# The last stores of a decoder step: one residual product, four vector adds, the sample rows and one store change their place

## The chip, the cores and the metric

The kernel runs on one core of a Trainium2 chip. The metric is the device time of one execution in microseconds (us). A core has TensorE (PE: matmuls, with its own weight loads, PEld), VectorE (DVE), ScalarE (ACT), GpSimd (POOL) and SyncE (SP), which here issues most DMAs. Every engine works through its own list of instructions in order and waits on semaphores; the program is over when all of them have reached the closing barrier.

## The reference, cut to what matters

One layer of a decoder is computed for 512 prompt tokens and 8 sample tokens (`D_MODEL` = 1024, all fp32): token mixing with sparse attention and gating, then a mixture of 32 experts with two experts for each token. Only the last sum touches the change:

```python
xp = xp + gate1 * merge_branches(...)                       # x2 in the kernel
xp = xp + gate2 * hierarchical_moe(modulate(xp, ...), ...)  # output y_prompt, (1, 512, 1024)
xs = xs + gate2 * hierarchical_moe(modulate(xs, ...), ...)  # output y_sample, (8, 1, 1024)
# hierarchical_moe: each token's output is the gated sum of its two experts' outputs
```

## The kernel before, in words

After token mixing the kernel sorts (token, choice) pairs into blocks of 64 rows, one expert each (`N_MAIN` = 35 blocks, and overflow blocks that run only where an expert got too many tokens). For each block POOL gathers the rows, PE computes gate, up and down products, DVE scales the result (`y_scaled`, L2697) and POOL scatters it to DRAM (`expert_rows`), into one place for each token and choice. 34 blocks are scattered so; the last one (label `LAST_LABEL`) isn't fetched back from DRAM for the prompt rows, but added by matmuls.

The end of the kernel, which the change touches, goes like this (t counts the four prompt tiles of 128 tokens, h the two halves of 512 columns):

- SP, once the scatters have landed (L1465), issues eight loads of 512 KB, `picked[c][t]` for choice c and tile t (L1468), in the order t = 0 to 3, and for each t choice 1, then choice 0. Behind them it waits for the last scatter (`s_scattered`) and issues two small loads of the sample rows (L1471, `s_picked`).
- PE adds the residual `x2` and the last block's rows in PSUM: `last_residual(t, h)` (L1337) is a product of the identity with `x2`, 128 rows by 512 columns; `last_tile(t)` calls `last_rows` (L1341) for both halves, products of a one-hot 64-row matrix with the last block's output, in the upper and the lower half of the array. Each fp32 product shows as two MATMUL records. `last_rows` of t = 0 waits for `y_out` of the last block (L1367), that is for DVE's L2697. Tile 3 is filled and drained by halves.
- ACT copies each finished tile from PSUM back into `x2` (L1687: tiles 0 to 2 whole, tile 3 by halves).
- DVE adds the two picks of a tile (`picks_summed(t)`, L2751), then the tile that ACT copied (`last_added(t)`, L2756; for tile 3 by halves, L2769). `last_added` first waits for all marked DVE operations before it (`lane.wait()`). Behind these come three small operations that make the sample rows (L2774 to L2776, 128 x 64): sum of the two choices, times gate, plus residual.
- SP stores tiles 0 to 2 (L1474), the halves of tile 3 (L1478) and the sample rows (L1480), each when its sum is ready, and waits for all to land before it goes to the closing barrier.
- PE, ACT, POOL and SP also run `over_pairs` (L587): a loop of two turns (L590) whose body, the overflow blocks, is skipped by a branch (L591) where there are none. PE runs it at its very end, after it has waited for ACT to drain every bank of the last tiles (L1379); ACT runs it at its end too; POOL after the last scatter (L1640); SP before the loads of L1468.
- L278 is the helper line of the closing barrier: a DRAIN on every engine, then the semaphores on which they meet.

The order in every engine's list is written out by hand.

Of the kernel before, what the change touches and what calls it, by code (L numbers as in the profile page):

```python
# [20 lines left out]
ALU = mybir.AluOpType  # L21
# [7 lines left out]
NT = SEQ // P  # L29
# [246 lines left out]
def decoder_step(nc, io):  # L276
    ctx = ExitStack()
    with ctx:  # L278
# [3 lines left out]
        def sem(name):  # L282
            return ctx.enter_context(nc.semaphore(name))
# [13 lines left out]
        def at(offset, size):  # L297
            return arena[:, offset:offset + size]
# [123 lines left out]
        s_cols = at(5120, 4 * Q_S).rearrange("p (m n) -> p m n", m=4)  # L422
# [69 lines left out]
        s_picked = (const2_in, 32 + 32)  # L492
# [6 lines left out]
        s_back = (x_in[NT], 16 + 32)  # L499
# [18 lines left out]
        outs, y_outs = sem("outs"), sem("y_outs")  # L518
# [44 lines left out]
        y_s_ready = (new_spread_ready, 2)  # L563
# [14 lines left out]
        def sample_columns(rows):  # L578

            return rows.rearrange("b (q n) -> (b q) n", q=16)  # L580
# [6 lines left out]
        def over_pairs(engine, pair):  # L587

            n_steps = engine.value_load(step_count[0:1, 0:1], min_val=0, max_val=N_OVER_STEPS)
            with engine.Fori(0, N_OVER_STEPS) as i:  # L590
                with engine.If(i < n_steps):  # L591
                    for q in range(OVER_AT_ONCE // 2):
                        pair(lambda per_pair, more: i * (per_pair * OVER_AT_ONCE // 2) + (per_pair * q + more))
# [13 lines left out]
        def pair(b0):  # L607

            return psum[:, b0:b0 + 2, 0:HALF]
# [7 lines left out]
        def _(pe):  # L617
# [415 lines left out]
            for g in range(2):  # L1033
                for h in range(2):
                    a = 2 * g + h
# [229 lines left out]
            def down(p, w, full):  # L1265
                for f in range(2):
                    for half in range(2):
                        mm = pe.matmul(psum[SB * half:SB * half + SB, 6 + p, :], hidden_T[:, p, f, :],  # L1268
                                       w[:, f, 512 * half:512 * half + 512], start=(f == 0), stop=(f == 1),
                                       tile_position=(0, SB * half))  # L1270
                mm.then_inc(full, 1)
# [8 lines left out]
            for b in range(N_SCATTERED + 1):  # L1280
                p = b % 2
                if b < N_SCATTERED:
                    pos, _, first, _ = BLOCKS[b]
                    if first:
                        pe.wait_ge(gu_got[pos % BUFFERS], 16 * (pos // BUFFERS + 1))
                    pe.wait_ge(xT_out, b + 1)
                    if b >= 2:
                        pe.wait_ge(hidden_done, b - 1)
                    if b == 3:
                        over_items()  # L1290
                    gate_up(p, w_gu[pos % BUFFERS], gu_full)
                    if b == 0:
                        gate_items()
                        over_code()
                    elif b == 2:
                        over_sums()
# [11 lines left out]
                if b >= 1:  # L1308
                    pos, _, first, _ = BLOCKS[b - 1]
                    if first:  # L1310
                        pe.wait_ge(dn_got[pos % BUFFERS], 16 * (pos // BUFFERS + 1))
                    pe.wait_ge(hT_out, b)
                    if b == 2:
                        banks.wait_drained(pe, "gate_items")
                    if b >= 3:
                        pe.wait_ge(y_out, b - 2)
                    down(1 - p, w_dn[pos % BUFFERS], y_full)
# [14 lines left out]
            def last_residual(t, h):  # L1332

                if h == 0 or t == NT - 1:
                    name = ("last", t, h) if t == NT - 1 else ("last", t)
                    banks.begin(pe, name, *((LAST_BANK[t] + h,) if t == NT - 1 else (LAST_BANK[t], LAST_BANK[t] + 1)))
                pe.matmul(psum[:, LAST_BANK[t] + h, :], ident, x2[:, t, 512 * h:512 * h + 512], start=True, stop=False)  # L1337
# [6 lines left out]
            def last_tile(t):  # L1344
                last_rows(t, 0)
                banks.filled(last_rows(t, 1), ("last", t))
# [14 lines left out]
            pe.wait_ge(y_out, b - 1)  # L1361
            down(LAST_P, w_dn[k], y_full)
            last_residual(1, 0)


            pe.wait_ge(last_hot_ready, 3)
            pe.wait_ge(y_out, N_MAIN)  # L1367
            last_tile(0)
            last_residual(1, 1)
            last_tile(1)  # L1370
            for h in range(2):
                last_residual(2, h)
# [11 lines left out]
        def _(sp):  # L1384
# [87 lines left out]
            for t in range(NT - 1):  # L1472
                sp.wait_ge(y_ready, t + 1)
                sp.dma_start(io["y_p"][t * P:(t + 1) * P, :], picked[0][t]).then_inc(y_outs, 16)  # L1474
            for h in range(2):
                cols = slice(512 * h, 512 * h + 512)
                sp.wait_ge(y_ready, NT + h)
                sp.dma_start(io["y_p"][(NT - 1) * P:NT * P, cols], picked[0][NT - 1][:, cols]).then_inc(y_outs, 16)  # L1478
            sp.wait_ge(*y_s_ready)
            sp.dma_start(sample_columns(io["y_s"]), s_cols[:, 2, :]).then_inc(y_outs, 16)  # L1480
            sp.wait_ge(y_outs, 16 * (T5 + 1))

        @block.gpsimd
        def _(pool):
            lane = Lane(pool, pool_lane)
# [186 lines left out]

            pool.wait_ge(over_ready, 1)
            over_pairs(pool, pool_pair)
            pool.wait_ge(outs, 16 * n_outs[0])

        @block.scalar
        def _(act):
# [59 lines left out]
            def products_out(name):  # L1738
                width = max(o + w for _, o, w, _ in slices[name])
                evac((name, "s"), [(G[:, 1, 0:width], psum[:, 2, 0:width])])  # L1740
# [168 lines left out]
            for i, (_, n, t) in enumerate(ORDER):  # L1909
                if i == 0:  # L1910
                    banks.wait_full(act, ("adaS", 8))
                square_half(i, n, t, 0, x2_half)
                if i == 3:
                    banks.wait_full(act, ("O0", "S"))
                    evac(("O1", "s"), [(G[:, 1, :], psum[:, 2, :])])
# [116 lines left out]
        def _(dve):  # L2032
            lane = Lane(dve, vector_lane)
# [662 lines left out]
            def y_scaled(p, done):  # L2696
                dve.tensor_tensor(y_rows[:, p, :], psum[:, 6 + p, :], y_rows[:, p, :], ALU.mult).then_inc(done, 1)  # L2697
# [50 lines left out]
            def picks_summed(t):  # L2748
                for c in (1, 0):
                    dve.wait_ge(*picked_in[c][t])  # L2750
                lane.mark(dve.tensor_tensor(picked[0][t], picked[0][t], picked[1][t], ALU.add))  # L2751

            def last_added(t):
                banks.wait_drained(dve, ("last", t))
                lane.wait()
                dve.tensor_tensor(picked[0][t], picked[0][t], x2[:, t, :], ALU.add).then_inc(y_ready, 1)  # L2756

            dve.wait_ge(y_full, b + 1)
            y_scaled(LAST_P, y_out)
            for t in range(NT):  # L2760
                picks_summed(t)
                if t < NT - 1:
                    last_added(t)
            for h in range(2):
                cols = slice(512 * h, 512 * h + 512)
                banks.wait_drained(dve, ("last", t, h))
                if h == 0:
                    lane.wait()
                dve.tensor_tensor(picked[0][t][:, cols], picked[0][t][:, cols], x2[:, t, cols], ALU.add).then_inc(y_ready, 1)  # L2769

            a, gate2, x = s_cols[:, 2, :], s_cols[:, 0, :], s_cols[:, 1, :]
            dve.wait_ge(*s_back)
            dve.wait_ge(*s_picked)
            lane.then(dve.tensor_tensor(a, a, s_cols[:, 3, :], ALU.add))  # L2774
            lane.then(dve.tensor_tensor(a, a, gate2, ALU.mult))
            dve.tensor_tensor(a, a, x, ALU.add).then_inc(y_s_ready[0], 1)  # L2776


# [90 lines left out]
```

## Time and profile before

| | us |
|---|---|
| device time, median of 3 runs | 794.43 (794.12 to 795.21) |
| device time of the profiled execution | 794.43 |
| its span, first to last instruction | 792.7 |
| PE busy | 744.3 (94%) |
| DVE, ACT, POOL busy | 407.6, 210.9, 169.6 |
| granted TensorE clock, mean | 0.985 |

The span is what the trace covers; about 1.8 us of the device time lie around it. Times in the rows are us from the span's start, where not marked ns. A row such as `773.47 1.13 PE L1337 ... x2` says: from 773.47, busy for 1.13 us, two instructions of line 1337. Names with a q behind the engine (SPq, PEldq) are what the engine's sequencer does itself: waits, branches, register loads, DMA issues.

### The profile page before, as it was taken

The numbers are of one execution on the slowest core, as the hardware profiler recorded it, in microseconds if no ns is written. First come the engines' busy times: TensorE is split into PE (matmuls) and PEld (weight loads), VectorE is DVE, ScalarE is ACT, GpSimd is POOL, SyncE is SP. The second block draws the span as 40 slices with busy tenths as digits, with TensorE's granted clock in tenths as the row PEclk, the third lists the DMA queues.
The fourth block names the chain that finished last, engine by engine and source line by source line (L and its number), as shares of the span: only waits on it lengthen the run. The fifth ranks groups of instructions, "written<-read, shape, count | busy, mean of one in ns | idle before, by whom it ended". The sixth has DMA issues, their size and how long they took to land.

```text
span 792.7 us, 11139 instructions
## 1 busy us (share of the span) xinstructions
PE 744.3 (94%) x4235; PEld 457.9 (58%) x4235; DVE 407.6 (51%) x940; ACT 210.9 (27%) x426; POOL 169.6 (21%) x193
## 2 busy tenths in 40 slices
PE   4999999999999989999999999987999999999886
PEld 3444465588766656887888344555555555555431
DVE  4124299998999989600214523883433232232225
ACT  4013243415366866103000211221111111111102
POOL 2030012051000000064400002454233333333210
PEclk9999999999999999999999999997999999999999
DMA  8962032533056444243132822148999999999987
GB/s 343 420 192 93 1 106 74 212 120 111 27 211 239 162 172 159 98 154 137 61 107 80 342 110 107 55 171 358 421 431 422 422 429 424 424 427 419 425 335 274
DMA packets 26832, 183.80 MB, mean 232 GB/s; under 512 B 6960, under 2 KB 7384, under 8 KB 15384
## 3 DMA queue, kind: packets, MB, share of 16 engines
q1 hardware_dynamic: 16328, 161.06, 50.2%
q0 software_dynamic: 9536, 19.72, 7.5%
q10 hardware_dynamic: 912, 2.26, 0.8%
q8 instruction: 36, 0.59, 0.3%
q14 instruction: 20, 0.16, 0.1%
HBM read 178.66 MB, written 14.44 MB: 244 GB/s over the span
## 4 chain that ended last, share of the span: by engine, by line
PE 79%; DMA 9%; ACT 4%; DVE 4%; issue 2%; POOL 1%; SPq 0%; DVEq 0%; POOLq 0%; ACTq 0%
PE psum L764 22%; PE psum L1254 13%; PE psum L731 11%; PE psum L1268 7%; DMA arena<-in_experts 5%; PE psum L695 3%; PE psum L641 3%; PE psum L1247 2%; DMA ring<-in_stream 2%; ACT arena L1687 2%; DMA arena<-in_cache_ki,stat 1%; PE psum L1155 1%; PE psum L949 1%; PE psum L624 1%; PE psum L960 1%
## 5 line engine op out<-in xcount | busy, mean ns | idle before, releaser
L764 PE MATMUL psum<-hT,ring 128*128 128x260 f32 x640 | 143.8, 384 | 0.9 <-issue 0.5
L1687 ACT ACTIVATE arena<-psum 128x512 f32<-128x512 f32 (+10 forms) x135 | 73.1, 576 | 236.0 <-PE psum L764 56.4
L764 PEld LDWEIGHTS psum<-hT,ring 128*128 128x128 f32 x640 | 120.5, 190 | 23.6 <-issue 4.4
L731 PE MATMUL psum<-ring,hT 128*128 128x512 f32 (+1 forms) x256 | 94.6, 523 | 0.0
L731 PEld LDWEIGHTS psum<-ring,hT 128*128 128x128 f32 x256 | 47.8, 192 | 43.7 <-issue 34.9
L1254 PE MATMUL psum<-ring,arena 128*64 128x256 f32 x608 | 70.7, 386 | 1.9 <-DMA ring<-in_experts 1.2
L1268 PE MATMUL psum<-arena 128*64 128x512 f32 x280 | 67.8, 605 | 1.4 <-issue 1.4
L1619 POOL DMA_INDIRECT expert_rows<-arena,router x34 | 34.5, 1014 | 142.0 <-DVE arena L2697 129.7
L1254 PEld LDWEIGHTS psum<-ring,arena 128*64 128x64 f32 x608 | 44.5, 140 | 32.2 <-issue 11.3
L2690 DVE COPY arena<-psum 128x128 f32<-128x128 f32 x35 | 10.2, 291 | 98.2 <-PE psum L1261 80.1
L1980 ACT ACTIVATE arena<-psum 64x256 f32<-64x256 f32 x35 | 13.4, 382 | 172.2 <-PE psum L1254 92.5
L764 PE MATMUL psum<-arena,ring 128*128 128x260 f32 x256 | 58.6, 391 | 0.0
L764 PEld LDWEIGHTS psum<-arena,ring 128*128 128x128 f32 x256 | 49.6, 194 | 7.9
L2697 DVE TENSOR_TENSOR arena<-psum,arena 128x512 f32<-128x512 f32 x35 | 24.2, 691 | 47.3 <-PE psum L1268 47.3
L1548 POOL DMA_INDIRECT arena<-in_cache_k,arena x16 | 15.4, 960 | 148.6 <-DVE arena L2331 141.2
L1254 PE MATMUL psum<-arena 128*64 128x256 f32 x352 | 40.0, 380 | 2.5 <-DMA arena<-in_experts 1.7
L1613 POOL DMA_INDIRECT arena<-t_rows,router x35 | 35.9, 1026 | 17.9 <-issue 10.1
L2194 DVE MAX8 arena<-arena 40x8 f32<-40x1025 f32 x32 | 38.7, 1211 | 0.7 <-issue 0.2
L2195 DVE FIND_INDEX8 arena<-arena 40x8 uint32<-40x1025 f32 x32 | 38.8, 1211 | 0.0
L2196 DVE MATCH_REPLACE8 arena<-arena 40x1025 f32<-40x1025 f32 x32 | 38.5, 1204 | 0.0
L1254 PEld LDWEIGHTS psum<-arena 128*64 128x64 f32 x352 | 25.5, 137 | 19.8 <-issue 5.6
L1268 PEld LDWEIGHTS psum<-arena 128*64 128x64 f32 x280 | 17.1, 136 | 27.7 <-issue 27.4
(395 smaller groups left out, 953.7 us busy)
## 6 DMA issues: line engine op xcount, KB each, us to landing
ring<-in_stream SPq DMA_DIRECT2D x21, 2048.0 KB, 8.3
ring<-in_experts SPq DMA_DIRECT2D x16, 2048.0 KB
arena<-in_experts SPq DMA_DIRECT2D x32, 1024.0 KB
arena<-in_experts SPq DMA_DIRECT2D x11, 2048.0 KB
hT<-in_experts SPq DMA_DIRECT2D x5, 2048.0 KB
ring<-expert_rows SPq DMA_DIRECT2D x8, 512.0 KB, 7.7
ring<-in_stream SPq DMA_DIRECT2D x2, 1280.0 KB, 6.0
arena<-in_x_prompt SPq DMA_DIRECT2D x4, 512.0 KB, 6.0
```

The lines of the kernel that those rows point to most:

```text
L641: mm = pe.matmul(psum[32 * j:32 * j + 32, b, :], c_T[:, 4 * h + j, :], w[:, 4 * h + j, :], start=(h == 0), stop=(h == 1), tile_position=(0 ...
L731: mm = pe.matmul(psum[:, b, 0:width], hT[:, k, t * P:(t + 1) * P], w[:, k, :], start=(k == 0), stop=(k == KD - 1))
L764: mm = pe.matmul(psum[:, b0 + s, 0:HALF], w[:, k, f * P:(f + 1) * P], rhs[:, k, s * HALF:(s + 1) * HALF], start=(first and k == 0), stop=( ...
L1254: mm = pe.matmul(psum[SB * half:SB * half + SB, 2 + p, 0:DE], x_T[:, p, k, :], w[:, 4 * (k % 2) + k // 2, col:col + DE], start=(k == 0), s ...
L1268: mm = pe.matmul(psum[SB * half:SB * half + SB, 6 + p, :], hidden_T[:, p, f, :], w[:, f, 512 * half:512 * half + 512], start=(f == 0), sto ...
L1613: pool.indirect_dma_start(x_rows[:, b % X_BUFFERS, :], None, half_rows, bass.IndirectOffsetOnAxis(token_tab[:, label:label + 1], 0), bound ...
L1619: pool.indirect_dma_start(picks, bass.IndirectOffsetOnAxis(dest_tab[:, label:label + 1], 0), y_rows[:, b % 2, :], None, bounds_check=4 * T ...
L1687: ins = act.activation(out, in_, func, scale=scale)
L2194: lane.then(dve.max(best, s))
L2195: lane.mark(dve.max_index(idx_u[0:32 + NS, 8 * r:8 * r + 8], best, s))
L2196: lane.then(dve.match_replace(s, best, s, TAKEN))
L2697: dve.tensor_tensor(y_rows[:, p, :], psum[:, 6 + p, :], y_rows[:, p, :], ALU.mult).then_inc(done, 1)
```

## The change

Five edits, all in the last 20 us:

- PE: `last_residual(1, 1)` moves from behind `last_tile(0)` to ahead of the wait for `y_out`, so that it follows `last_residual(1, 0)`.
- DVE: the order of picks sums (P) and last adds (A) by tile, before P0 A0 P1 A1 P2 A2 P3, becomes P0 P1 P2 A0 A1 P3 A2; the two halves of tile 3 follow as before.
- The three operations of the sample rows leave DVE's list and stand in POOL's, behind its `over_pairs`, with their waits.
- SP: the store of the sample rows moves ahead of the stores of tile 3's halves, with its wait for `y_s_ready`.
- Semaphores and buffers stay as they were.

```diff
             down(LAST_P, w_dn[k], y_full)
             last_residual(1, 0)
+            last_residual(1, 1)
 
             pe.wait_ge(last_hot_ready, 3)
             pe.wait_ge(y_out, N_MAIN)
             last_tile(0)
-            last_residual(1, 1)
             last_tile(1)
...
                 sp.dma_start(io["y_p"][t * P:(t + 1) * P, :], picked[0][t]).then_inc(y_outs, 16)
+            sp.wait_ge(*y_s_ready)
+            sp.dma_start(sample_columns(io["y_s"]), s_cols[:, 2, :]).then_inc(y_outs, 16)
             for h in range(2):
...
-            sp.wait_ge(*y_s_ready)
-            sp.dma_start(sample_columns(io["y_s"]), s_cols[:, 2, :]).then_inc(y_outs, 16)
...
             over_pairs(pool, pool_pair)
+
+            a, gate2, x = s_cols[:, 2, :], s_cols[:, 0, :], s_cols[:, 1, :]
+            pool.wait_ge(*s_back)
+            pool.wait_ge(*s_picked)
+            lane.then(pool.tensor_tensor(a, a, s_cols[:, 3, :], ALU.add))
+            lane.then(pool.tensor_tensor(a, a, gate2, ALU.mult))
+            pool.tensor_tensor(a, a, x, ALU.add).then_inc(y_s_ready[0], 1)
...
-            for t in range(NT):
-                picks_summed(t)
-                if t < NT - 1:
-                    last_added(t)
+            picks_summed(0)
+            picks_summed(1)
+            picks_summed(2)
+            last_added(0)
+            last_added(1)
+            picks_summed(3)
+            last_added(2)
+            t = NT - 1
             for h in range(2):
...
-
-            a, gate2, x = s_cols[:, 2, :], s_cols[:, 0, :], s_cols[:, 1, :]
-            dve.wait_ge(*s_back)
-            dve.wait_ge(*s_picked)
-            lane.then(dve.tensor_tensor(a, a, s_cols[:, 3, :], ALU.add))
-            lane.then(dve.tensor_tensor(a, a, gate2, ALU.mult))
-            dve.tensor_tensor(a, a, x, ALU.add).then_inc(y_s_ready[0], 1)
```

## Rows read from the trace of the kernel before

**Rows 1.** Chain that ended last, from 784 us: start, duration, what.

```profile
783.90 1.07 PE psum L1341 x2
...
786.74 0.23 DVE arena L2776
```

**Rows 2.** Waits of SP, from 765 us: total us, times, longest.

```profile
SPq L278 <- PEq L278: 2.6, 1, 2.6
SPq L278 <- DMA out_y_s<-arena: 2.5, 1, 2.5
```

**Rows 3.** Line 278, the closing barrier: duration ns min/median/max, first and last start.

```profile
L278 POOLq DRAIN  x1: 9303/9303/9303, 777.4 to 777.4; - x1
...
L278 SPq COMPARE_BRANCH  x1: 37/37/37, 789.9 to 789.9; - x1
...
L278 PEldq DRAIN  x1: 8/8/8, 792.4 to 792.4; - x1
```

**Rows 4.** Lines 589 and 591, loop count and skipping branch, same columns.

```profile
L589 PEldq TENSOR_LOAD <-router x1: 1080/1080/1080, 785.7 to 785.7; - x1
...
L591 ACTq COMPARE_BRANCH  x2: 50/52/55, 786.2 to 787.1; - x2
L591 PEldq COMPARE_BRANCH  x2: 232/2076/3920, 787.4 to 791.9; - x2
```

**Rows 5.** Timeline of PE from 773 us: start, busy, engine, line, what.

```profile
773.47 1.13 PE L1337 MATMUL psum<-arena,const 128*128 128x512 f32 x2
774.52 1.13 PE L1341 MATMUL psum<-arena 64*128 64x512 f32 x4
775.58 1.13 PE L1337 MATMUL psum<-arena,const 128*128 128x512 f32 x2
...
777.70 1.98 PE L1337 MATMUL psum<-arena,const 128*128 128x512 f32 x4
779.61 1.13 PE L1341 MATMUL psum<-arena 64*128 64x512 f32 x4
```

**Rows 6.** Timeline of DVE and ACT, 774 to 787 us; in brackets idle and releaser.

```profile
774.19 1.22 DVE L2751 TENSOR_TENSOR ring<-ring 128x1024 f32<-128x1024 f32 x1
...
776.75 1.23 DVE L2756 TENSOR_TENSOR ring<-ring,arena 128x1024 f32<-128x1024 f32 x1 [1.35 <-ACT arena L1687]
...
784.99 0.60 ACT L1687 ACTIVATE arena<-psum 128x512 f32<-128x512 f32 x1 [1.51 <-PE psum L1341]
...
785.62 0.69 DVE L2769 TENSOR_TENSOR ring<-ring,arena 128x512 f32<-128x512 f32 x1 [0.62 <-ACT arena L1687]
786.23 0.22 DVE L2774 TENSOR_TENSOR arena<-arena 128x64 f32<-128x64 f32 x1
```

**Rows 7.** Timeline of SP's DMA issues, same columns.

```profile
782.37 1.74 SPq L1474 DMA_DIRECT2D out_y_p<-ring  x3
...
787.00 0.36 SPq L1480 DMA_DIRECT2D out_y_s<-arena  x1
```

**Rows 8.** Lines 1468 and 1471: issue ns, first and last start, and time to landing.

```profile
L1468 SPq DMA_DIRECT2D ring<-expert_rows x8: 341/440/943, 769.0 to 772.4; - x8
...
DMA to landing us min/median/max: 3.8/7.7/9.9
...
L1471 SPq DMA_DIRECT2D arena<-expert_rows x2: 319/376/432, 781.5 to 781.9; - x2
...
DMA to landing us min/median/max: 1.6/1.8/1.9
```

**Rows 9.** Windows of and behind the stores: us, busy of PE, PEld, DVE, ACT, POOL, clock, DMA share, GB/s.

```profile
783.30:788.90 5.60, 1.66 (x4) 0.29 (x2) 2.87 (x6) 0.78 (x2) 0.00 (x0) 1.00 1.00 383
...
788.90:792.70 3.80, 0.00 (x0) 0.00 (x0) 0.00 (x0) 0.00 (x0) 0.00 (x0) 0.57 0.03 6
```

**Rows 10.** POOL's groups of instructions: count, busy us, mean ns, idle before.

```profile
L1572 POOL TENSOR_TENSOR arena<-arena 128x1024 f32<-128x1024 f32 x4 | 9.4, 2346 | 4.2 <-DVE arena L2460 4.2
...
L1581 POOL TENSOR_TENSOR router<-router 128x1 f32<-128x1 f32 x4 | 0.8, 191 | 0.3
```

## The prediction

> **What bounds the kernel now.** I read the chain of waits first, because all five edits lie in the last 20 us. It follows TensorE up to the last product of line 1341 (783.90 to 784.97), then ScalarE's copy and VectorE, and stops at the third sample operation at 786.74 [rows 1]. Taken at its word, the sample rows and the store behind them are the end. But the span is 792.7, so nearly 6 us lie behind the chain's last piece, and the chain doesn't say whose they are. So the second view is what SP waits for. It waits 2.5 us for the last store, and then 2.6 us more for TensorE's sequencer at the closing barrier [rows 2]. The third view, the barrier's own line, puts times to it: SP leaves its wait for the stores at 789.9, TensorE reaches its DRAIN only at 792.4, and 0.2 us later all is over [rows 3]. TensorE is the last engine, by about 2.3 us.
>
> What does TensorE do after its last product? Its wait for ScalarE's last copy (784.99 plus 0.60) [rows 6] ends at 785.6; then comes the register load for the loop count (1.08 us from 785.7), and at 787.4 the branch that skips the overflow blocks, which takes 3.92 us; its second branch takes 0.23. ScalarE's same two branches take 0.05 each [rows 4]. So the end is made of this chain: last product, ScalarE's copy, and a tail of 792.4 - 785.6 = 6.8 us in TensorE's sequencer. Stores, VectorE and the sample rows run beside that tail.
>
> **The change part by part.** The sums are made against the profiled execution: span 792.7, device time 794.43, which happens to be the median too, so 1.8 us outside the span are carried over unchanged.
>
> *PE, one residual product earlier.* From 773.47 TensorE never stops: each group starts as the one before lets it, 1.05 to 1.06 us apart where full-array products (1337) and half-array products (1341) alternate [rows 5]. The wait for `y_out` costs nothing today: VectorE's L2697 is through at 774.3, while the residual of 773.47 runs to 774.52. With two residual products ahead it is further off the path. No product is added or taken away. What changes is who stands beside whom. Two residual groups side by side exist in the rows: the pair of 777.70 gives way to the next group at 779.61, 1.91 us, where two separate ones take 2 x 1.055 = 2.11. One such pair more saves 0.20 us. The edit also puts `last_tile(0)` beside `last_tile(1)`, half-array groups back to back, which these rows don't show. Bounds: nothing gained or lost, if their alternating weights keep the 1.06 us; 0.20 gained, if it is like the residual pair. I take 0.20, since the nearest row is that pair and the number of changes between the two kinds falls from four to two there. Sum on TensorE: 0.20 + 0.20 = 0.40 us, range 0.20 to 0.40. The last product ends at 784.57. Tile 0 is filled 0.85 us later than before, tile 1 0.2 to 0.4 earlier.
>
> The Trainium skill, TensorEngine Tiling (Array Packing), section Key Properties, says that a change of tiling mode drains the array. By this rule the tile pair saves the same 0.20 us as the residual pair, and the sum is 0.40; without it 0.20. The rows' 2.11 against 1.91 agree with it.
>
> *ScalarE.* Its copies follow TensorE; the last moves from 784.99 to 784.6 and ends at 785.2 [rows 6]. Nothing else enters its list.
>
> *TensorE's tail.* Same instructions, same count in front of the branch, 6.8 us, so its DRAIN comes at 792.0. The one thing that can stretch it is the 3.92 us branch. The stores are in flight beside it: from 783.3 to 788.9 the DMA engines are fully busy at 383 GB/s [rows 9]. The Trainium skill, Runtime: NRT & Kernel Launch, section Instruction fetch mechanics, says that a taken branch to code outside the window held forces a DMA fetch before execution goes on; the branch's 3.92 us against 0.05 on an engine with a short body [rows 4] agrees. By this rule the stall depends on DMA traffic, and I price that as a rival below.
>
> *VectorE, new order.* A picks sum needs two loads of 512 KB. The eight land between 769.0 + 3.8 = 772.8 and 772.4 + 9.9 = 782.3 [rows 8], one every 9.5/7 = 1.36 us; so the pairs are complete at about 774.2, 776.9, 779.6 and 782.3. In the old order A0 (776.75) fills the gap between them [rows 6]. In the new one P1 runs from about 777 and P2 from 779.7 to 780.9, with VectorE idle in between, and only then A0 (to 782.3), A1 (to 783.4), P3 (to 784.6), A2 (784.7 to 785.9), the halves at 785.8 and 786.4, the last done at 787.1. Before, it was 785.62 + 0.69 = 786.3. So the last prompt sum comes 0.8 us later, although three operations of 0.22 us leave VectorE's list. Who waits for that is SP alone.
>
> *POOL.* Its three operations wait for the sample loads: 781.9 + 1.9 = 783.8 [rows 8]. POOL is free since 777.4 [rows 3]. No row has a 128 x 64 one. Lower bound 0.19 us each (128 x 1), upper 2.35 us each (128 x 1024) [rows 10]. I go between them by size, 0.19 + 2.16 x 64/1024 = 0.33, with a small gap 1.1 us in all: ready at 784.9. Upper end: 783.8 + 7.1 = 790.9.
>
> *SP.* Two waits change place. The sample store now stands ahead of tile 3's halves, and its wait holds both of them. New times: A0 at 782.4, A1 at 783.4, A2 at 785.9 (the three stood behind one another from 782.37 to 784.1), sample rows 786.4 (was 787.0) [rows 7], halves 786.8 and 787.2. The stream then has 1.05 MB left from A2 on; at 383 GB/s that is 2.7 us, from some 1 us after its issue: 787.0 to 789.7, landed by 790.2, perhaps 790.8. Before, 789.9. So SP reaches the barrier 0.3 to 0.9 us later, but still 1.2 us or more before TensorE's 792.0. Cost zero, and the cover is TensorE's tail; without it this part would be a loss of 0.3 to 0.9 us.
>
> Sum: 792.7 - 0.4 = 792.3 span, and 794.43 - 0.40 = **794.0 us** of device time. That is 0.05%. A measurement of this kernel can tell about 0.2% (1.6 us) from no change, so the forecast is "no measurable change".
>
> **The rivals.**
>
> 1. *The stores set the end* (the chain's picture). Then the time follows the last landing, 0.3 to 0.9 us later by the sum above: 795.0. For it: the chain stops in the sample rows [rows 1]. Against it: SP's 2.6 us wait for TensorE [rows 2]. Chance 0.05.
>
> 2. *The branch meets the store stream.* It now starts at 787.0 instead of 787.4, and the stream ends at 789.7 instead of 788.9. If what the branch fetches waits behind the stores, it ends 0.8 us later than before instead of 0.4 earlier: 794.43 + 0.8 = 795.2. For it: the branch spans the end of the stream. Against it: the 2.4 us of the branch that lie behind 788.9 are spent on an idle DMA system [rows 4, 9], so most of the stall is no queueing. Chance 0.12.
>
> 3. *The slower side: POOL is late.* The three operations at their upper end are ready at 790.9; SP, blocked in front of tile 3's halves, then issues three stores, the last landing about 3.0 us later, 793.9, and SP is in the barrier at 794.1 instead of TensorE at 792.0. Against the old 792.4 that is +1.7: 796.1. It decides over TensorE from a ready time of about 788.8, which is 1.7 us for each operation, and loses against the kernel before from 789.2. For it: POOL's DRAIN of 9.3 us in the old tail, ending only at 786.7 [rows 3], which no row explains; if it blocked the three operations too, they would be ready at 787.8, and SP would be in the barrier at about 791.1: still no loss. Against it: 0.19 us for a small operation [rows 10]. Chance 0.06.
>
> The Trainium skill, GPSIMD Engine Reference, section Key points, says that POOL's SBUF interfaces are shared with VectorE where VectorE has two SBUF inputs, as all its sums here have. By this rule the operations stretch towards rival 3, and no row here prices a 128 x 64 one beside such sums.
>
> 4. *The tail shrinks*: the fetch finds the code or the branch is short, up to 3.7 us off TensorE, when the stores become last at 790.8: 794.43 - 1.6 = 792.8. Nothing in the list of TensorE speaks for it. Chance 0.03.
>
> **How the numbers follow.** Forecast 0.74: 794.0, its own range 793.6 to 794.5. Rivals 1 and 2 (0.17) lie at 795.0 and 795.2 and are within 0.2% too, as the forecast is. Rival 3 reaches 796.1 only at its far end. The range takes the forecast with rivals 1 and 2 and the scatter of the runs shown: 793.4 to 795.4. Faster by over 0.2%: rival 4 and scatter, 0.06. Slower by over 0.2%: the far end of rival 3 and scatter, 0.07. Between them 0.87.
>
> **What would show it.** TensorE: two residual groups at 773.5 to 775.4, two tile groups behind them in 1.9 us, the last product at 784.6, its DRAIN last at about 792.0, SP again waiting for it, now 1.2 to 1.8 us. VectorE: idle before the second and the third picks sum, its last sum done near 787.1. POOL: three operations of some 0.3 us from 783.8. SP: tile 2's store at 785.9. Wrong would be: SP's or POOL's DRAIN last; a branch that isn't within 0.5 us of 3.9; tile groups 1.06 us apart; or device time outside 793.4 to 795.4.

## The result, and the profile after

The changed kernel is slower: 798.09 us median (796.3 to 803.18, 17 runs) against 794.43 (791.22 to 797.62, 17 runs) of the kernel before; ratio 1.0053, 95% interval 1.0038 to 1.0067. The forecast was 794.0 and "no measurable change"; both the size and the range were missed.

One thing is needed to read the traces. The time ahead of the change differs from run to run: VectorE's last `y_scaled` ends anywhere from 767.9 us (e6) to 776.6 us (e8) in traces whose lists are alike up to the last blocks, so a span by itself says little. I therefore count from the end of this `y_scaled`, around which the changed lists begin, and call the rest the tail. It ends at 774.27 in the trace before and at 771.63 after:

```profile
773.58 0.69 DVE L2697 TENSOR_TENSOR arena<-psum,arena 128x512 f32<-128x512 f32 x1 [2.59 <-PE psum L1268]
```

```profile
770.94 0.69 DVE L2704 TENSOR_TENSOR arena<-psum,arena 128x512 f32<-128x512 f32 x1 [2.59 <-PE psum L1268]
```

The spans are 792.66 and 793.58, so the tail is 18.4 us before and 21.9 after: 3.6 us longer, 0.45% of the run, which lies within the interval of the ratio. (The second profiled run had reached its tail 2.6 us sooner, by scatter, and so shows a span only 0.9 longer.)

The closing barrier of the changed kernel, in the columns of [rows 3]:

```profile
L278 POOLq DRAIN  x1: 9847/9847/9847, 783.5 to 783.5; - x1
L278 ACTq DRAIN  x1: 8/8/8, 784.6 to 784.6; - x1
...
L278 SPq DRAIN  x1: 13/13/13, 789.3 to 789.3; - x1
L278 PEldq DRAIN  x1: 8/8/8, 789.4 to 789.4; - x1
```

TensorE reaches its DRAIN at 789.4 and SP at 789.3, 17.8 and 17.7 us into the tail. POOL's DRAIN is issued at 783.5 and ends at 793.3, and 0.2 us later all is over. Before, a DRAIN of 9.30 us stood at 777.4 and ended at 786.7 [rows 3], in the shadow of TensorE's tail. It is the same DRAIN; it now starts behind the sample rows:

```profile
772.47 1.45 POOL L1640 DMA_INDIRECT expert_rows<-arena,router  x1 [7.51 <-DVE arena L2704]
781.11 0.84 POOL L1679 TENSOR_TENSOR arena<-arena 128x64 f32<-128x64 f32 x1 [7.20 <-DMA arena<-expert_rows]
782.03 1.25 POOL L1680 TENSOR_TENSOR arena<-arena 128x64 f32<-128x64 f32 x1
783.36 0.65 POOL L1681 TENSOR_TENSOR arena<-arena 128x64 f32<-128x64 f32 x1
```

From the third operation's end (784.01) to the DRAIN's end (793.34) it is again 9.33 us. (It is listed with 9.85 us because it is issued 0.5 us before the third operation ends.) The operations themselves take 2.9 us with their gaps, not 1.1.

SP's list of waits names another engine than POOL:

```profile
SPq L278 <- PEq L278: 4.2, 1, 4.2
SPq L278 <- DMA out_y_p<-ring: 3.7, 1, 3.7
```

Such a line can mislead. Before, the same line named TensorE too, for 2.6 us [rows 2], and TensorE was indeed last [rows 3]. Here it still names TensorE, though TensorE had been there for 4 us. Only the DRAIN rows, start and length of each engine, tell the two apart.

TensorE and VectorE went almost as forecast:

```profile
770.82 1.98 PE L1337 MATMUL psum<-arena,const 128*128 128x512 f32 x4
772.74 1.99 PE L1341 MATMUL psum<-arena 64*128 64x512 f32 x8
774.65 1.98 PE L1337 MATMUL psum<-arena,const 128*128 128x512 f32 x4
```

Both pairs now take 1.91 to 1.92 us from start to start, where [rows 5] had 1.05 to 1.06 for each single group; the last product ends 10.28 us into the tail instead of 10.68. Two steps behind it changed, which the forecast had as constant:

```profile
L589 PEldq TENSOR_LOAD <-router x1: 522/522/522, 782.7 to 782.7; - x1
```

```profile
L591 PEldq COMPARE_BRANCH  x2: 227/2398/4568, 783.8 to 788.9; - x2
```

The register load of the loop count took 0.52 us instead of 1.08, and the branch 4.57 instead of 3.92 [rows 4].

VectorE:

```profile
771.84 1.23 DVE L2758 TENSOR_TENSOR ring<-ring 128x1024 f32<-128x1024 f32 x1 [0.20 <-DMA ring<-expert_rows]
774.39 1.22 DVE L2758 TENSOR_TENSOR ring<-ring 128x1024 f32<-128x1024 f32 x1 [1.33 <-DMA ring<-expert_rows]
776.95 1.23 DVE L2758 TENSOR_TENSOR ring<-ring 128x1024 f32<-128x1024 f32 x1 [1.34 <-DMA ring<-expert_rows]
...
783.02 1.53 DVE L2780 TENSOR_TENSOR ring<-ring,arena 128x512 f32<-128x512 f32 x2
```

VectorE idles 1.3 us ahead of the second and the third picks sum, waiting for the loads, where it did a last add in between before [rows 6]. Its last prompt sum ends 12.9 us into the tail instead of 12.0.

### The profile page after: what moved, and what is told of

Its sections match the earlier page's. It is cut to its first block, busy times and chain, and to the rows that moved or that the text cites. A ratio compares the mean times of both kernels' runs of the same rounds, so it can differ in the third digit from the quotient of the medians.

```text
span 793.6 us, 11139 instructions
## 1 busy us (share of the span) xinstructions
PE 742.2 (94%) x4235; PEld 457.2 (58%) x4235; DVE 407.3 (51%) x937; ACT 211.1 (27%) x426; POOL 172.5 (22%) x196
## 4 chain that ended last, share of the span: by engine, by line
PE 75%; DMA 11%; ACT 4%; DVE 4%; issue 3%; POOL 1%; SPq 1%; DVEq 0%; POOLq 0%; ACTq 0%
PE psum L764 21%; PE psum L1254 12%; PE psum L731 10%; PE psum L1268 7%; DMA ring<-in_experts 5%; PE psum L695 3%; PE psum L641 3%; PE psum L1247 2%; DMA ring<-in_stream 2%; ACT arena L1694 2%; PE psum L949 1%; PE psum L1155 1%; DMA arena<-in_cache_ki,stat 1%; PE psum L960 1%; PE psum L624 1%
## 5 line engine op out<-in xcount | busy, mean ns | idle before, releaser
L764 PE MATMUL psum<-arena,ring 128*128 128x260 f32 x256 | 56.9, 384 | 0.0
L1268 PEld LDWEIGHTS psum<-arena 128*64 128x64 f32 x280 | 17.2, 136 | 27.7 <-issue 27.5
```

What stands on the lines that cost most here:

```text
L764: mm = pe.matmul(psum[:, b0 + s, 0:HALF], w[:, k, f * P:(f + 1) * P], rhs[:, k, s * HALF:(s + 1) * HALF], start=(first and k == 0), stop=( ...
```

## The experiments

Ratios are to the kernel before, timed beside it on the same chip, each with its 95% interval; tails are from one trace each. Two traces in which TensorE's list and the stores are the same put its DRAIN at 18.14 (before) and 18.11 us (e4), so I read differences of some 0.1 us in a tail as nothing. e9 to e11 ran once each and have no ratio. In the diffs, lines in parentheses stand for several lines of code.

| run | edit | ratio | tail |
|---|---|---|---|
| changed kernel | | 1.0053 (1.0038 to 1.0067) | 21.9 |
| e1 | changed, sample rows back on VectorE | 0.9981 (0.9960 to 1.0001) | 18.4 |
| e2 | before, sample rows on POOL | 1.0030 (1.0007 to 1.0053) | 20.9 |
| e3 | changed, DRAIN ahead of the sample rows | 1.0002 (0.9987 to 1.0017) | 18.5 |
| e4 | before, POOL waits for the sample loads | 1.0006 (0.9988 to 1.0024) | 19.0 |
| e5 | before, TensorE's tail cut | 0.9992 (0.9974 to 1.0010) | 16.9 |
| e6 | e5 and TensorE's new order | 0.9972 (0.9953 to 0.9990) | 17.1 |
| e7 | e6 and VectorE's new order | 0.9995 (0.9972 to 1.0018) | 17.2 |
| e8 | e6, sample rows ahead of the halves | 0.9990 (0.9971 to 1.0009) | 17.2 |
| e9 | before, DRAIN ahead of the last scatter | - | 19.0 |
| e10 | before, TensorE's new order alone | - | 17.9 |
| e11 | before, VectorE's new order alone | - | 18.7 |
| e12 | changed, DRAIN in the expert loop | 1.0060 (1.0037 to 1.0083) | 21.2 |

**e1_sample_on_dve**

```diff
-            (three sample operations on pool)
+            (the same on dve, behind the halves of tile 3; sample store last on sp)
```

> The changed kernel with the three sample operations back on VectorE and the sample store back at the end; TensorE's and VectorE's new orders stay. 'Tail' is the time from VectorE's last y_scaled to the span's end: 18.4 us before, 21.9 in the changed kernel. Theory A (POOL's closing DRAIN lasts some 9.3 us from its last operation and now ends last): POOL's DRAIN starts early again and ends about 12.4 us after y_scaled; the end is TensorE's again, tail 18.0 to 18.5, device time 0.1 us slower to 0.4 us faster than before. Theory B (VectorE's new order and the later stores are the loss): tail stays near 21.9, 3 us or more slower than before.

Measured: ratio 0.9981, tail 18.4.

```profile
L278 POOLq DRAIN  x1: 9303/9303/9303, 771.5 to 771.5; - x1
...
L278 SPq DRAIN  x1: 13/13/13, 786.4 to 786.4; - x1
L278 PEldq DRAIN  x1: 8/8/8, 786.5 to 786.5; - x1
```

POOL's DRAIN starts 3.1 us into the tail, takes 9.303 us and ends at 12.4. TensorE's DRAIN (18.17) is last, SP's (18.04) just ahead. Theory B falls: with both new orders kept the loss is gone.

**e2_pool_only**

```diff
             over_pairs(pool, pool_pair)
+            (waits, three sample operations)      # and taken from dve
```

> The kernel before with one edit: the three sample operations go to POOL, everything else in its old order. Theory A: POOL's last operation ends 10 to 12.5 us after y_scaled, its DRAIN takes 9.3 more, tail 20 to 22, device time 2 to 4 us slower. Theory B: within 0.5 us of before.

Measured: ratio 1.0030, tail 20.9.

```profile
L278 POOLq DRAIN  x1: 9518/9518/9518, 784.5 to 784.5; - x1
...
L278 SPq DRAIN  x1: 13/13/13, 789.0 to 789.0; - x1
L278 PEldq DRAIN  x1: 8/8/8, 791.3 to 791.3; - x1
```

This edit alone makes the loss, 2.5 us of the 3.6. The other 1.1 come from the operations being later: the last ends 11.3 us into the tail here and 12.4 in the changed kernel (they start 0.3 us later there, and take 0.84, 1.25 and 0.65 us, with VectorE's sums beside them, where they take 0.88, 0.72 and 0.32 here).

**e3_early_drain**

```diff
             over_pairs(pool, pool_pair)
+            pool.drain()
```

> The changed kernel with an explicit DRAIN on POOL behind over_pairs, ahead of the sample operations. Theory A1 (the 9.3 us belong to the indirect DMAs and are paid once): the early DRAIN takes about 9 us, ends some 12.4 us after y_scaled, the sample operations follow, the closing DRAIN is short, and the end is TensorE's or SP's, tail 18 to 19. Theory A2 (every late DRAIN of POOL costs 9.3 us, whatever came before): two DRAINs of 9.3 us, tail 24 to 26, some 6 us slower than before. Theory B: tail stays at 21.9 or grows by what POOL's delay adds.

Measured: ratio 1.0002, tail 18.5. The waiting is paid once:

```profile
L1675 POOLq DRAIN  x1: 9303/9303/9303, 775.9 to 775.9; - x1
```

```profile
L278 POOLq DRAIN  x1: 268/268/268, 786.5 to 786.5; - x1
L278 PEldq DRAIN  x1: 8/8/8, 790.7 to 790.7; - x1
...
L278 SPq DRAIN  x1: 13/13/13, 791.2 to 791.2; - x1
```

One line more turns the 0.5% loss into no change. It doesn't make a gain: the sample rows now start behind the DRAIN, 12.4 us into the tail, SP waits 1.8 us for them, and SP's barrier comes at 18.3.

**e4_pool_waits**

```diff
             over_pairs(pool, pool_pair)
+            pool.wait_ge(*s_back)
+            pool.wait_ge(*s_picked)
```

> The kernel before, where POOL only waits for the loads of the sample rows (about 9.5 us after y_scaled) ahead of its DRAIN and does nothing behind the wait. If the DRAIN counts from its own issue, it ends 9.5 + 9.3 = 18.8 us after y_scaled and the tail is 19.0, 0.6 us over before. If it counts from POOL's last operation (the indirect DMA), it ends at 12.4 as before and the tail stays at 18.4. Theory B has no difference either.

Measured: ratio 1.0006, tail 19.04, forecast 19.0.

```profile
L278 POOLq DRAIN  x1: 9303/9303/9303, 783.7 to 783.7; - x1
...
L278 PEldq DRAIN  x1: 8/8/8, 792.4 to 792.4; - x1
```

POOL ran no operation for 7.5 us, and the DRAIN is 9303 ns long all the same. It counts from its own issue; time passed idle doesn't shorten it. (The ratio can't tell 0.6 us from nothing; this rests on the trace.) A wait alone, without work behind it, puts POOL last.

**e5_pe_tail**

```diff
             gate_up(LAST_P, w_gu[k], gu_full)
+            pe.wait_ge(over_ready, 1)
+            n_steps = pe.value_load(step_count[0:1, 0:1], ...)
...
-            (waits for the drained banks; over_pairs with its own value_load)
+            with pe.Fori(0, N_OVER_STEPS) as i:
+                with pe.If(i < n_steps):
+                    (waits for the drained banks; the pairs)
```

> The kernel before, with TensorE's tail cut: it reads the loop count right behind the last gate_up, and its waits for ScalarE's drains stand inside the skipped loop body. All other lists are as before. Tail is the time from VectorE's last y_scaled to the span's end, 18.4 us before. Theory A (the end before is TensorE's tail; next is SP's wait for the stores, 15.8 us after y_scaled): TensorE's branch starts some 3 us earlier, its DRAIN comes at 14 to 15, the end is SP's, tail 15.8 to 16.3, 2.1 to 2.6 us faster than before. Theory C (the branch ends when the stream of stores lets its code through, whenever it starts): the branch still ends near 16.7 to 17.0 and the tail is 18.0 to 18.3.

Measured: tail 16.9 (ratio 0.9992, which doesn't tell 1.5 us from nothing). Theory C falls: the branch starts 3.6 and ends 9.0 us into the tail. But it takes longer:

```profile
L1381 PEldq COMPARE_BRANCH  x2: 233/2782/5330, 777.6 to 783.5; - x2
```

5.33 us beside a busy stream, 3.92 before [rows 4]; the products queued ahead hide it. Theory A is right in who is last (SP, at 16.65) and 0.6 us or more too fast: SP's issues of the halves took 0.63 and 0.75 us instead of 0.33, and the stores landed later.

**e6_pe_tail_pe_order**

```diff
+            last_residual(1, 1)        # on top of e5, as in the change
```

> As e5_pe_tail, and last_residual(1, 1) ahead of the wait for y_out. Theory A: TensorE's last product ends at 10.3 instead of 10.7 us after y_scaled, the last half tile and the sample rows come 0.4 earlier, SP ends at about 15.4, tail 15.5 to 16.0. Theory C: no difference from e5.

Measured: ratio 0.9972, the one version whose interval lies wholly below the kernel before. Its tail, 17.1, is no shorter than e5's, where 15.5 to 16.0 was expected:

```profile
779.38 2.03 SPq L1482 DMA_DIRECT2D out_y_p<-ring  x2
781.45 0.43 SPq L1484 DMA_DIRECT2D out_y_s<-arena  x1
```

The two issues of the halves took 0.33 and 1.43 us, and the last store landed at 16.7. The tail's 1.3 us are 0.16% of the run, which the ratio's interval holds; nothing beyond them is shown. The tails of e5 and e6 are alike, so the difference between their ratios is not shown to be the order's.

**e7_pe_tail_both_orders**

```diff
+            (VectorE's new order)      # on top of e6
```

> As e6_pe_tail_pe_order, and VectorE's new order P0 P1 P2 A0 A1 P3 A2 (sample rows on VectorE, at the end). With TensorE's tail out of the way the price of this order shows: SP's wait for the stores ended 18.0 us after y_scaled with it (e1) against 15.8 in the old order, so the tail is 17.5 to 18.4, about 2 us over e6 and no faster than the kernel before. If the order were free, it would equal e6.

Measured: ratio 0.9995, tail 17.2, shorter than expected. The 2 us that I expected the order to cost don't show; SP ends at 17.0, as in e6 (16.9).

**e8_best**

```diff
+            (on dve: sample operations between P3 and the halves)   # on top of e6
+            (on sp: sample store ahead of the halves' stores)
```

> As e6_pe_tail_pe_order, with VectorE's old order and the three sample operations on VectorE between the third picks sum's successor (P3) and the halves of tile 3; the sample store goes ahead of the halves' stores. Theory A: sample rows ready at 10.7 instead of 12.7 us after y_scaled, the last half at 11.9, the last store lands near 15.0, tail 15.2 to 15.7, some 3 us faster than before: the version that beats both kernels.

Measured: ratio 0.9990, tail 17.2: a miss. The sums are ready sooner, but the last landing stays at 16.8. In e5 to e8 it lies at 16.5 to 16.8, whatever the order of the sums.

**e9_drain_before_last_scatter**

```diff
             scatter(N_SCATTERED - 1)
+            pool.drain()
             pool.wait_ge(last_dest_ready, 2)
```

> The kernel before with one more DRAIN on POOL, ahead of the last scatter, so that a single indirect DMA lies between it and the closing DRAIN. If the 9.3 us grow with the number of indirect DMAs since the last DRAIN (94 in the kernel), the first takes some 9.2 us and the closing one well under 1 us. If they are fixed once any indirect DMA has run, both take 9.3 us: the first starts about 7 us before y_scaled ends, delays the last scatter by 1 to 2.5 us, and the closing one ends near 13 to 15 us after y_scaled.

Measured: the first DRAIN takes 10.4 us, the closing one 2.1. (The count in the expectation is wrong: the kernel issues 111 indirect DMAs, 8 + 32 + 35 + 36.)

```profile
L1638 POOLq DRAIN  x1: 10432/10432/10432, 763.4 to 763.4; - x1
```

```profile
L278 POOLq DRAIN  x1: 2123/2123/2123, 777.0 to 777.0; - x1
```

Neither expectation holds. The length depends on what lies before the DRAIN, since the last one; a single indirect DMA doesn't bring the 9.3 us back. The last scatter came 2.6 us later for the first DRAIN, and the tail is 0.6 us longer.

**e10_pe_order_only**

```diff
+            last_residual(1, 1)        # and taken from behind last_tile(0)
```

> The kernel before with TensorE's edit alone. The last product ends at 10.3 instead of 10.7 us after y_scaled. Theory A': the branch has to fetch its code through the stream of stores; it starts 0.4 us earlier and ends at 16.7 to 17.0 all the same, so that the tail is 18.1 to 18.4 (18.4 before). If the branch were a fixed 3.9 us, the tail would be 18.0.

Measured: last product at 10.28, branch 3.79 us, tail 17.87. The edit is worth 0.5 us in this trace: 0.40 from the earlier product, as forecast, and 0.13 from a branch that was shorter. Theory A' falls here, where VectorE's sums and the stores are in the old order.

**e11_dve_order_only**

```diff
-            P0 A0 P1 A1 P2 A2 P3
+            P0 P1 P2 A0 A1 P3 A2
```

> The kernel before with VectorE's new order alone. Last half tile stored about 0.8 us later, sample rows behind it; SP's wait ends at 17.5 to 18.3 us after y_scaled instead of 15.8, and TensorE's DRAIN at 18.1 to 18.3: the cover of this edit is nearly used up, tail 18.3 to 18.6. If the order cost only the 0.3 to 0.9 us of the prediction, SP's wait would end at 16.1 to 16.7.

Measured: tail 18.7.

```profile
L591 PEldq COMPARE_BRANCH  x2: 233/2546/4860, 785.2 to 790.6; - x2
```

```profile
L278 SPq COMPARE_BRANCH  x1: 38/38/38, 790.5 to 790.5; - x1
L278 SPq DRAIN  x1: 13/13/13, 790.6 to 790.6; - x1
```

SP's wait ends at 17.8 (15.6 before), and TensorE's branch takes 4.86 us instead of 3.92; the packet with its code starts 1.0 us later in it (last section), while the stores run. Its DRAIN comes at 18.5.

**e12_after_drain_in_loop**

```diff
                     scatter(b - 1)
+                if b == N_SCATTERED - 3:
+                    pool.drain()
```

> The changed kernel with one more DRAIN on POOL, in the expert loop behind the scatter of block 30, so that four indirect DMAs are left for the closing one. Theory A3 (a DRAIN pays for the indirect DMAs since the last one; 2.1 us for one in e9, 9.3 for all): the DRAIN in the loop takes 9 to 10 us and is hidden by the 7.5 us blocks and double-buffered rows; the closing DRAIN takes 2 to 4 us and ends 14.5 to 16.5 us after y_scaled, TensorE and SP are last again, tail 17.9 to 18.4 instead of 21.9, some 0.5% faster than the changed kernel and within 0.2% of before. If the price were 9.3 us whenever more than one indirect DMA has run, the tail stays at 21.5 to 22. If the DRAIN in the loop can't be hidden, the last blocks of the loop run 1 to 3 us late.

Measured: ratio 1.0060, tail 21.2, no repair. The mechanism holds and the remedy fails:

```profile
L278 POOLq DRAIN  x1: 1545/1545/1545, 792.6 to 792.6; - x1
L278 PEldq DRAIN  x1: 8/8/8, 795.9 to 795.9; - x1
...
L278 SPq DRAIN  x1: 13/13/13, 799.7 to 799.7; - x1
```

The closing DRAIN ends 0.4 us behind the last operation, so POOL is no longer last. But the one in the loop took 12.0 us, the scatters and the loads behind it came late, and SP stored everything some 3 us later:

```profile
789.90 4.06 SPq L1474 DMA_DIRECT2D out_y_p<-ring  x3
794.00 0.43 SPq L1476 DMA_DIRECT2D out_y_s<-arena  x1
794.47 1.28 SPq L1480 DMA_DIRECT2D out_y_p<-ring  x2
```

## Why the prediction was wrong

- **The step that failed is the one on POOL.** It put the cost of the moved operations at their own time: "ready at 784.9", with a cover up to 788.8. It counted what waits for them on SP, and not what stands behind them in POOL's own list. That is the closing DRAIN, which has to come after them and takes 9.3 us. In the trace before, POOL's slack was not the 15 us from 777.4 to 792.4 but 792.4 - 786.7 = 5.7 us. The operations moved the DRAIN by 12.4 - 3.1 = 9.3 us and used up 3.6 us more than there was. The row was on the table [rows 3]; rival 3 took it for a delay that might end at a fixed time and block the operations, instead of one that follows them. e2 shows it by this edit alone, e4 by the DRAIN alone without the operations, and e1 and e3 by taking the late DRAIN away. With the forecast's own 1.1 us for the operations the DRAIN would still have ended at 784.9 + 9.3 = 794.2, 1.8 us behind TensorE's old 792.4: the DRAIN left out makes the loss, the operations' size adds to it.
- **POOL's operations** were mis-sized: 2.9 us with their gaps instead of 1.1, 0.65 to 1.25 us each. Alone they take 0.32 us (the second and third of e3), which is what I had interpolated; beside VectorE's sums of two SBUF inputs they stretch up to four times. The trace agrees here with the Trainium skill, GPSIMD Engine Reference, section Key points, which says that POOL shares its SBUF interfaces with VectorE and contends with VectorE's instructions that have two SBUF inputs.
- **TensorE**: right, 0.40 us for the two pairs, and the last product at 10.28 us. In e10 it shortens the tail.
- **TensorE's tail**: the 6.8 us that I called constant are not. The register load ahead of the branch took 0.56 us less in the changed kernel, so that with the 0.40 of the products the branch started 1.0 us earlier; but it took 4.57 us instead of 3.92, so its end moved by only 0.3. The 0.3 against the forecast 0.4 is partly luck: one change that I did not foresee made up for the other. Rival 2 was partly right, and its counter-argument was wrong: of the 3.92 us before, 1.5 passed until the packet with its code started, while the DMA engines were 91% busy (last section).
- **VectorE's order**: right in mechanism and in size on VectorE itself (0.9 us later, forecast 0.8). What follows on SP was too small: its barrier came 1.9 us later (17.7 against 15.8), forecast 0.3 to 0.9. The cover was TensorE's tail, and only 0.1 us of it was left. By itself the edit lengthened the tail by 0.35 us in one trace (e11), through TensorE's branch; with TensorE's tail cut it cost nothing that shows (e7, 17.2 against 17.1).
- **The sum**: by TensorE's tail the changed kernel would have ended 0.3 us sooner; POOL's 3.9 us over TensorE make it 3.6 us later. e1's trace, without the late POOL, has a tail equal to that of before, so the mean gain that its ratio suggests isn't shown by the tail.

## What to carry to other kernels

Count the slack of an engine from the end of its last instruction, and the closing DRAIN is one: read the start and the length of every engine's DRAIN before moving work to the engine that looks idle. Where POOL's closing DRAIN is long, and work has to go behind its last wait, have it drain before that wait, so that the long DRAIN runs while POOL has nothing to do (e3, which undid the loss but made no gain), and not in a loop that depends on it (e12). When several engines end within some 2 us of each other, taking one away uncovers the next: in e5 TensorE was done 7.4 us sooner, and the tail was 1.5 us shorter.

## What the runs showed of the hardware

- POOL's DRAIN took 9303 ns, to the nanosecond, in ten traces (before, e1, e3 to e8, e10, e11), whether it started 3 or 9.5 us into the tail. It took 10.4 and 12.0 us where it stood between scatters (e9, e12), 0.27 us where another DRAIN had come just before (e3), 2.1 us with one indirect DMA between (e9), and ended 0.4 us behind the last operation with four of them, the last 13 us back (e12). What it waits for stays open: the number of indirect DMAs since the last DRAIN doesn't order these lengths, and POOL also issued 23 plain DMAs, whose share no run tells apart.
- TensorE's taken branch over the skipped body cost 3.7 (e2) to 6.0 us (e8). In each of the 14 traces one 16 KB packet of an instruction queue runs inside it, for 0.9 to 1.4 us, and the branch ends 1.4 us behind that packet (1.38 to 1.43). I infer that the branch is a wait for this packet. What varies is the time until it starts: 1.3 us in e2, 1.5 before, 1.8 in the changed kernel, 2.5 in e11, 3.6 in e8. The DMA engines were 70% to 100% busy in that time. Their share over the whole branch doesn't tell its length (0.74 for 3.88 us in e12, 0.64 for 6.04 in e8).
- The last increments of the stores' semaphore straggle. Of the last sixteen, ten or more come within 0.2 us, and the last few up to 2 us behind them: the sixteen spread over 1.8 to 2.2 us in e1, e9 to e12 and the changed kernel, over 0.8 before and in e2, e4 and e7, and over 0.3 in e3. The cause is open. TensorE's instruction packet is not enough for one: before, it runs at 14.6 us of the tail too, with a spread of 0.75, and in e5, e6 and e8 it is over by 13 us and the spread is 1.4 to 1.6.
